# Six buffers for gathered expert rows in place of eight, and query weights in the memory of the other two

## The chip, the cores and the metric

The kernel runs on one core of one Trainium2 chip. The metric is the device time of one execution in microseconds. A NeuronCore has a matrix engine (TensorE, PE in the profile), a vector engine (VectorE, DVE), a scalar engine (ScalarE, ACT), GpSimd (POOL) and SyncE (SP). The last two issue most of this kernel's transfers; all transfers of the core run on the same 16 DMA engines. On-chip memory has 128 partitions.

## What is computed

One block with convolution, windowed attention and a retrieval of experts ("peer"), followed by two further blocks with attention and feed-forward parts, all on 256 tokens of width 1024 in float32. The part that the change touches is the expert retrieval:

```python
q = (h @ w_pq).reshape(B, S, PEER_HEADS, 2, PEER_DHALF)      # 8 heads, 2 x 128
sc = jnp.einsum("bshcd,hcnd->bshcn", q, sub_keys)            # 128 keys per half
s_top, i_top = lax.top_k(sc, 16)
# all 16 x 16 sums of the two halves, of which the best 16 name 16 experts
a = gelu(jnp.einsum("ced,cd->ce", u_emb[idx], hx))           # one dot per expert
out = jnp.einsum("ce,ced->cd", g * a, v_emb[idx])            # weighted sum of rows
```

Each token picks 8 x 16 = 128 experts out of 16384. For each it needs a row of `u_emb` and a row of `v_emb`, 1024 floats each, which lie side by side in one array `uv`.

## The kernel before

**Rows of experts.** Tokens lie on the partitions, in two tiles of 128. For each tile and each of its 128 expert slots, POOL issues one indirect DMA (line 751) that brings 128 rows of 2048 floats (1 MB) into one of `NROWS = 8` buffers of `gath`, a view of the memory `pool` from offset 0. These are 256 gathers, numbered n in the code, here called rows. DVE forms the dot of the first half with the token's normed activations (line 2242). ACT handles two rows at a time: gelu (L1660), product with the gate (L1664), a diagonal matrix from each coefficient (L1670). PE multiplies the diagonal with the second half of the row and sums in PSUM (L1221). When PE is through with row n, `row_spent` rises, and POOL may issue gather n + 8 (`wait_spent(gp, n - NROWS)`).

**What stands between the rows.** Each group of 16 rows belongs to one head of one tile. While they are worked, DVE selects the experts of the head two groups later, in nine steps. ACT computes the exponentials of the gates once per group, which needs another table than gelu. PE projects queries and scores of heads 2 to 7 at fixed rows, written in `QUERY_SLOTS`: projections at rows 0, 8, 19, 30, 42 and 54, scores at 2, 14, 25, 36, 48 and 60. Heads 0 and 1 are done ahead of the stage. In the second tile PE also runs three token projections of the next block (`TOKEN_SLOTS`, rows 159, 183 and 207 in all) on the first tile's result.

**Weights.** SP streams all weights as chunks of up to 2 MB, in the order of `CHUNKS`, into a ring of three slots (line 698). Chunk n is loaded when chunk n - 3 has had its last use. The query weights are four chunks `pq` 0 to 3, two heads each. `pq` 2 is outside the ring: it is loaded early into four places that are free at that time. In the ring the order around the stage is convout 0 and 1, wout 0 and 1, pq 0, pq 1, pq 3, va, cqkv 0, cqkv 1, qa. `LAST_USE` names the fill after which each slot may be reused: for pq 0 the query of head 1, tile 1; for pq 1 the query of head 3 (row 8); for pq 3 that of head 7 (row 54).

**The start of the stage.** The experts of the first head come in two halves of eight. POOL waits for the first eight (`first_ranks`) ahead of gather 0. Buffers 0 to 3 lie below the copies of the output projection's weights in `pool` (`f_hi`, from offset 8432 on), buffers 4 to 7 over them. So POOL waits for the last output fill (`wout`, 1, 1) ahead of gather `ROWS_BELOW_WEIGHTS = 4`. The convolution's outputs `y_hi` and `y_lo` use `pool` from 0 to 4336 and are last read by the fill (`convout`, 1, 1).

Of the kernel before, what the change touches and what calls it, by code (L numbers as in the profile page):

```python
# [25 lines left out]
D = 1024  # L26
KD = D // P
# [15 lines left out]
LARGE = 3.0e38  # L43
TABLE_SCALE = 8.0
UNITS = NT * PH
NROWS = 8
NDIAG = 4
SELECT_STEPS = 9
SELECT_AT = (0, 2, 3, 5, 7, 8, 10, 12, 13)
# [27 lines left out]


EARLY_QUERY = 2


def chunk_list():
    out = [(("glu", i), 4096) for i in range(4)] + [(("q1", i), 4096) for i in range(2)] + [(("kv1", 0), 2048)]
    out += [(("gate", i), 4096) for i in range(4)]
    out += [(("attno", i), 4096) for i in range(2)] + [(("convout", i), 4096) for i in range(2)]
    out += [(("wout", i), 4096) for i in range(2)]
    out += [(("pq", i), 4096) for i in range(4) if i != EARLY_QUERY]
    out += [(("va", 0), 4096), (("cqkv", 0), 4096), (("cqkv", 1), 4096), (("qa", 0), 4096), (("ka", 0), 4096),
            (("kpe_uq", 0), 3328), (("uq_ukv", 0), 3584), (("evout", 0), 4096), (("evout", 1), 4096)]
    for layer in range(2):  # L90
        if layer:
            out += [(("uz", 0), 4096), (("vz", 0), 4096), (("qd", 0), 4096), (("kd", 0), 4096), (("vd", 0), 4096),
                    (("ws", 0), 1024), (("odout", 0), 4096), (("odout", 1), 4096)]
        out += [(("gu%d" % layer, i), 4096) for i in range(KF // 2)]
        out += [(("down%d" % layer, i), min(4, KF - 4 * i) * D) for i in range(-(-KF // 4))]
    return out
# [67 lines left out]
               30: ("pq", 5), 36: ("sc", 5), 42: ("pq", 6), 48: ("sc", 6), 54: ("pq", 7), 60: ("sc", 7)}  # L164
QUERY_LAG = 4
QUERY_COPY_AFTER = {n + (QUERY_LAG if n else 0): fill for n, fill in QUERY_SLOTS.items()}
ROWS_BELOW_WEIGHTS = 4
SELECT_FIRST_AT = (7, 8, 9, 10, 11, 12, 13, 14, 15)
TOKEN_CHUNKS = (("va", 0), ("cqkv", 0), ("cqkv", 1))
NORM_SLOT = 15  # L170
# [47 lines left out]
FILL_NO = {name: n for n, name in enumerate(FILLS)}  # L218
# [102 lines left out]
        self.scale, self.table, self.sinks, self.column = scale, table, sinks, column  # L321


def build(nc, stream, early_query, consts, t5const, params, rows, keys_in, late_rows, x_in, positions, t5_in, rpb_in, uv, out):
    with ExitStack() as ctx:
        def sb(name, shape, dt=F32):
            return ctx.enter_context(nc.sbuf_tensor(name, shape, dt))
# [1 line left out]
        def sem(name):  # L329
            return ctx.enter_context(nc.semaphore(name))  # L330
# [12 lines left out]
        pool = sb("pool", [P, 16384])  # L343
# [99 lines left out]

        qpT = view(att, 5120, 2, 2, S)
        keys = tab[:, :, :].rearrange("p h j -> p (h j)")[:, 0:2048].rearrange("p (m n) -> p m n", n=NKEYS)
        gath = view(pool, 0, NROWS, 2 * D)
        scores = view(att, 0, NT, 2 * PH * NKEYS)
        cand = att[:, 4096:4096 + TOPK * TOPK]
        first_cand = att[:, 1024:1024 + TOPK * TOPK]
# [38 lines left out]
        bank_filled = sem("bank_filled")  # L488
# [18 lines left out]
        row_landed = sem("row_landed")  # L507
        keys_landed = sem("keys_landed")
        early_query_landed = sem("early_query_landed")
        pos_landed = sem("pos_landed")  # L510
        t5_landed = sem("t5_landed")
        rpb_landed = sem("rpb_landed")
# [171 lines left out]
        @block.sync  # L684
        def _(sp):
            for t in range(NT):
                sp.dma_start(x[:, t, :], x_in[P * t:P * t + P, :]).then_inc(x_landed[t], 16)
            sp.dma_start(cst[:, :], consts).then_inc(const_landed, 16)
            sp.dma_start(par[:, :], params).then_inc(param_landed, 16)
            for n, (name, width) in enumerate(CHUNKS):  # L690
                if n >= NSLOT:
                    before = CHUNKS[n - NSLOT][0]
                    if before in LAST_PART:
                        wait_part_used(sp, *LAST_PART[before])
                    else:
                        sp.wait_ge(bank_filled, FILL_NO[last_use(before)] + 1)
                src = stream[CHUNK_AT[n]:CHUNK_AT[n + 1]].rearrange("(p w) -> p w", p=P)
                sp.dma_start(ring[:, n % NSLOT, 0:width], src).then_inc(chunk_landed[n % NSLOT], 16)
                if name == ("wout", 0):
                    sp.wait_ge(bank_filled, FILL_NO["attno", 1, 1] + 1)  # L700
                    sp.wait_ge(t5_stored, 16)
                    sp.wait_ge(rpb_stored, 16)
                    for c, piece in enumerate(query_pieces):
                        sp.dma_start(piece, early_query[:, 1024 * c:1024 * c + 1024].rearrange("p (k n) -> p k n", k=2)
                                     ).then_inc(early_query_landed, 16)
            for t in range(NT):
                sp.wait_ge(out_ready, t + 1)
                sp.dma_start(out[P * t:P * t + P, :], xn[:, t, :]).then_inc(out_stored, 16)
            sp.wait_ge(out_stored, 16 * NT)
# [69 lines left out]
        def _(pe):  # L779
# [404 lines left out]
            def query(kind, head):  # L1184
                dst = begin((kind, head))
                if kind == "pq":
                    if head // 2 == EARLY_QUERY:
                        pe.wait_ge(early_query_landed, 16 * len(query_pieces))
                        w = [query_pieces[k // 2][:, k % 2, :] for k in range(KD)]
                    else:  # L1190
                        chunk = wait_chunk(pe, ("pq", head // 2))[:, 0:4096].rearrange("p (k n) -> p k n", k=KD)
                        w = [chunk[:, k, :] for k in range(KD)]
# [51 lines left out]
            w = wait_chunk(pe, ("kpe_uq", 0))  # L1244
# [1261 lines left out]
```

## Time and profile before

| | us |
|---|---|
| three runs, median | 1607.2 |
| lowest, highest | 1601.48, 1609.42 |
| the profiled execution | 1604.03 |
| its span in the trace | 1602.1 |
| PE, DVE, ACT, POOL busy in the span | 1447.7, 1017.3, 646.3, 312.3 |
| moved by DMA | 428.59 MB, 268 GB/s on average |

The page lists busy time by engine, then the span in 40 slices of 40 us, each digit being tenths of a slice, then the chain of work that ended last and the costliest groups. Here the longest items of the chain are the landings of gathers (`pool<-uv,experts`, 19% of the span) and the three kinds of split matmuls (L933 to L935, 12% each). Idle time of an engine that is not the bound costs nothing; what matters of each stage is the wait that ends last in it.

### The profile page before, as it was taken

Reading aid. Unit: us, or ns where it says so; the run is one execution under the profiler, and the core shown is the slowest. Engines: PE = TensorE matmul, PEld = TensorE weight load, DVE = VectorE, ACT = ScalarE, POOL = GpSimd, SP = SyncE. Lnnn points to the kernel's source line nnn. Section 1 sums busy time; section 2 is a strip of 40 time slices with the busy share of each in tenths; the row PEclk is TensorE's granted clock in tenths of the full one; section 3 lists DMA queues with packets and bytes.
Section 4 is the critical chain, followed back from the end, with each engine's and each line's share of the span. In section 5 each row is a group of like instructions: output and inputs, shape, how many; then the busy total and the mean of one; then the engine's idle time right before and its main releaser. Section 6 shows DMA issues by size and latency. Waiting matters only on the chain.

```text
span 1602.1 us, 16913 instructions
## 1 busy us (share of the span) xinstructions
PE 1447.7 (90%) x6102; PEld 1002.6 (63%) x6102; DVE 1017.3 (63%) x1989; ACT 646.3 (40%) x1313; POOL 312.3 (19%) x298
## 2 busy tenths in 40 slices
PE   8998898989977777797987779989999999999998
PEld 6987897745533332333333237767888889878886
DVE  6999976767667777777665543346555455565553
ACT  4423662333333334433333224454444345544442
POOL 2000001144444444434434410400000000000000
PEclk9999999999999999999999999999999999999999
DMA  7546455999999999999999955413454444145451
GB/s 296 205 164 137 121 216 217 395 398 418 412 421 421 419 420 420 420 397 421 411 410 417 421 223 191 148 73 130 185 206 162 182 166 164 73 190 203 165 201 62
DMA packets 52212, 428.59 MB, mean 268 GB/s; under 512 B 6696, under 2 KB 6840, under 8 KB 10144
## 3 DMA queue, kind: packets, MB, share of 16 engines
q0 software_dynamic: 40464, 279.18, 43.7%
q1 hardware_dynamic: 11664, 148.33, 24.4%
q8 instruction: 49, 0.80, 0.2%
q14 instruction: 35, 0.29, 0.0%
HBM read 422.49 MB, written 4.98 MB: 267 GB/s over the span
## 4 chain that ended last, share of the span: by engine, by line
PE 62%; DMA 20%; DVE 10%; ACT 5%; issue 2%; POOL 0%; SPq 0%; DVEq 0%; ACTq 0%; POOLq 0%
DMA pool<-uv,experts 19%; PE psum L933 12%; PE psum L935 12%; PE psum L934 12%; PE psum L800 11%; PE psum L1221 10%; DVE pool L2242 3%; PE psum L834 2%; DVE pool L2010 2%; PE psum L880 1%; DVE ring_lo L1834 1%; ACT diag L1670 1%; ACT xn L1316 1%; DVE att L1811 1%; ACT coef L1664 1%
## 5 line engine op out<-in xcount | busy, mean ns | idle before, releaser
L1221 PE MATMUL psum<-pool,diag 128*128 128x512 f32 x1024 | 482.5, 621 | 109.9 <-ACT diag L1670 109.6
L1221 PEld LDWEIGHTS psum<-pool,diag 128*128 128x128 f32 x1024 | 194.7, 197 | 388.6 <-issue 213.0
L2242 DVE CUSTOM_DVE_ANT_0 pool<-pool,xn 128x1024 f32<-128x1024 f32 x256 | 313.4, 1226 | 195.8 <-DMA pool<-uv,experts 193.8
L751 POOL DMA_INDIRECT pool<-uv,experts x256 | 281.4, 1099 | 514.4 <-PE psum L1221 366.4
L1834 DVE TENSOR_TENSOR ring_lo<-ring,w_hi 128x2048 fp32r<-128x2048 f32 x76 | 174.0, 2292 | 114.0 <-ACT w_hi L1412 113.9
L1660 ACT ACTIVATE acts<-dots 128x2 f32<-128x2 f32 x128 | 26.0, 203 | 366.6 <-DVE dots L2242 366.4
L1412 ACT ACTIVATE w_hi<-ring 128x2048 fp32r<-128x2048 f32 x76 | 144.4, 1908 | 65.1 <-PE psum L935 36.0
L933 PE MATMUL psum<-w_hi,h_hi 128*128 128x512 f32 x400 | 161.2, 403 | 2.5 <-DVE ring_lo L1834 0.9
L934 PE MATMUL psum<-ring_lo,h_hi 128*128 128x512 f32 x400 | 157.2, 393 | 0.0
L935 PE MATMUL psum<-w_hi,h_lo 128*128 128x512 f32 x400 | 156.1, 390 | 0.0
L800 PE MATMUL psum<-hT,ring 128*128 128x256 f32 (+1 forms) x544 | 116.8, 376 | 0.8 <-issue 0.8
L800 PEld LDWEIGHTS psum<-hT,ring 128*128 128x128 f32 x544 | 100.2, 201 | 16.5 <-issue 3.1
L2010 DVE SCALAR_TENSOR_TENSOR pool<-pool,par 128x256 f32<-128x256 f32 x240 | 98.3, 486 | 0.2
L1670 ACT ACTIVATE diag<-cst,coef 128x128 f32<-128x128 f32 x256 | 89.6, 394 | 9.3 <-PE psum L1221 5.0
L933 PEld LDWEIGHTS psum<-w_hi,h_hi 128*128 128x128 f32 x400 | 75.2, 188 | 21.5 <-issue 3.1
L935 PEld LDWEIGHTS psum<-w_hi,h_lo 128*128 128x128 f32 x400 | 75.2, 188 | 18.6
L934 PEld LDWEIGHTS psum<-ring_lo,h_hi 128*128 128x128 f32 x400 | 74.9, 187 | 15.3
L933 PE MATMUL psum<-w_hi,gu_hi 128*128 128x512 f32 x176 | 70.1, 398 | 0.0
L934 PE MATMUL psum<-ring_lo,gu_hi 128*128 128x512 f32 x176 | 69.0, 392 | 0.0
L935 PE MATMUL psum<-w_hi,gu_lo 128*128 128x512 f32 x176 | 68.7, 390 | 0.0
L1664 ACT ACTIVATE coef<-acts,gates 128x1 f32<-128x1 f32 x256 | 61.4, 287 | 4.2
L1312 ACT ACTIVATE pool<-psum 128x512 f32<-128x512 f32 (+1 forms) x47 | 23.1, 505 | 88.7 <-PE psum L800 62.1
(327 smaller groups left out, 2156.1 us busy)
## 6 DMA issues: line engine op xcount, KB each, us to landing
ring<-stream SPq DMA_DIRECT2D x65, 2048.0 KB, 7.7
pool<-uv,experts POOLq DMA_INDIRECT x256, 12.5
ring<-stream SPq DMA_DIRECT2D x3, 1024.0 KB, 4.8
t_scratch<-tab POOLq DMA_DIRECT2D x1, 2048.0 KB, 56.3
rpb_scratch<-tab POOLq DMA_DIRECT2D x1, 1792.0 KB, 23.1
ring<-stream SPq DMA_DIRECT2D x1, 1792.0 KB, 8.1
row<-rows POOLq DMA_DIRECT2D x1, 1672.0 KB, 11.3
ring<-stream SPq DMA_DIRECT2D x1, 1664.0 KB, 6.6
```

The costliest lines, as they stand in the source:

```text
L751: gp.indirect_dma_start(out=gath[:, n % NROWS, :], out_offset=None, in_=uv, in_offset=bass.IndirectOffsetOnAxis(ap=experts[:, n:n + 1], ax ...
L800: last = nc.tensor.matmul(dst, lhsT, rhs, start=(i == 0), stop=(i == len(pairs) - 1))
L933: nc.tensor.matmul(dst, lhsT[0], rhs[0], start=start, stop=False)
L934: nc.tensor.matmul(dst, lhsT[0], rhs[1], start=False, stop=False)
L935: return nc.tensor.matmul(dst, lhsT[1], rhs[0], start=False, stop=stop)
L1221: last = nc.tensor.matmul(psum[:, RB + half, :], diag[:, n % NDIAG, :], gath[:, n % NROWS, D + 512 * half:D + 512 * half + 512], start=k = ...
L1412: nc.scalar.activation(part_high(layer, q), part_raw(layer, q), ACT.Copy).then_inc(hi_split, 1)
L1664: ins = nc.scalar.activation(coef[:, b, j:j + 1], acts[:, b, j:j + 1], ACT.Copy, scale=gates[:, n:n + 1])
L1670: nc.scalar.activation(diag[:, n % NDIAG, :], ident, ACT.Copy, scale=coef[:, b, j:j + 1]).then_inc(diag_ready, 1)
L1834: V.tensor_tensor(part_low(layer, q), part_raw(layer, q), part_high(layer, q).bitcast(F32), ALU.subtract).then_inc(lo_split, 1)
L2010: ins = V.scalar_tensor_tensor(y[:, m, :], src, tap, y[:, m, :], ALU.mult, ALU.add)
L2242: ins = V.tensor_tensor_reduce(out=row_u, in0=row_u, in1=xn[:, n // SLOTS, :], scale=1.0, scalar=0.0, op0=ALU.mult, op1=ALU.add, accum_out ...
```

## The change

`NROWS` becomes 6: `gath` starts at offset 4096 of `pool`, and the first 4096 columns of it, the place of two buffers, hold the query weights `pq` 3 of heads 6 and 7. These leave the ring. They come as an input of their own and are loaded by SP right behind chunk pq 0, after a wait for (`convout`, 1, 1). PE takes them from there for heads 6 and 7 and waits for their own semaphore. `ROWS_BELOW_WEIGHTS` becomes 2, since only two buffers now lie below the copies of the weights. The number of DMAs and of computing instructions is the same. One SP wait is added; one ring position fewer is used, which shifts all later chunks by one slot.

```diff
-NROWS = 8
+NROWS = 6
...
+ROW_QUERY = 3
...
-    out += [(("pq", i), 4096) for i in range(4) if i != EARLY_QUERY]
+    out += [(("pq", i), 4096) for i in range(4) if i not in (EARLY_QUERY, ROW_QUERY)]
...
-ROWS_BELOW_WEIGHTS = 4
+ROWS_BELOW_WEIGHTS = 2
...
-        gath = view(pool, 0, NROWS, 2 * D)
+        gath = view(pool, 2 * 2 * D, NROWS, 2 * D)
+        row_weights = pool[:, 0:2 * 2 * D]
...
                 sp.dma_start(ring[:, n % NSLOT, 0:width], src).then_inc(chunk_landed[n % NSLOT], 16)
+                if name == ("pq", 0):
+                    sp.wait_ge(bank_filled, FILL_NO["convout", 1, 1] + 1)
+                    sp.dma_start(row_weights, row_query).then_inc(row_query_landed, 16)
                 if name == ("wout", 0):
...
                     if head // 2 == EARLY_QUERY:
                         pe.wait_ge(early_query_landed, 16 * len(query_pieces))
                         w = [query_pieces[k // 2][:, k % 2, :] for k in range(KD)]
+                    elif head // 2 == ROW_QUERY:
+                        pe.wait_ge(row_query_landed, 16)
+                        w = [row_weights[:, 512 * k:512 * k + 512] for k in range(KD)]
```

## Rows read from the trace of the kernel before

**Rows 1.** The page, DMA share and rate in 40 slices of 40 us.
```profile
DMA  7546455999999999999999955413454444145451
GB/s 296 205 164 137 121 216 217 395 398 418 412 421 421 419 420 420 420 397 421 411 410 417 421 223 191 148 73 130 185 206 162 182 166 164 73 190 203 165 201 62
```

**Rows 2.** Windows: length, busy PE, PEld, DVE, ACT, POOL, then PEclk, DMA, GB/s.
```profile
247.00:262.00 15.00, 14.23 (x82) 11.63 (x82) 6.41 (x24) 3.75 (x11) 0.00 (x0) 1.00 0.00 1
...
505.30:512.00 6.70, 5.74 (x7) 2.52 (x8) 4.93 (x17) 2.54 (x9) 1.35 (x1) 0.50 1.01 421
...
450.00:940.00 490.00, 388.45 (x828) 156.89 (x828) 335.28 (x811) 174.21 (x532) 207.23 (x190) 0.96 1.01 416
```

**Rows 3.** Line 751, the gathers issued from 880 to 926 us.
```profile
L751 POOL DMA_INDIRECT pool<-uv,experts x19: 943/943/1802, 881.1 to 926.0; - x19
...
DMA to landing us min/median/max: 12.2/12.7/13.5
```

**Rows 4.** Timeline of DVE, start and us; the dots of rows 249 and 253.
```profile
926.24 1.23 DVE L2242 CUSTOM_DVE_ANT_0 pool<-pool,xn 128x1024 f32<-128x1024 f32 x1 [1.15 <-DMA pool<-uv,experts]
...
936.22 1.23 DVE L2242 CUSTOM_DVE_ANT_0 pool<-pool,xn 128x1024 f32<-128x1024 f32 x1 [1.14 <-DMA pool<-uv,experts]
```

**Rows 5.** Timeline of PE, one pair of rows in an undisturbed stretch.
```profile
923.73 3.70 PE L1221 MATMUL psum<-pool,diag 128*128 128x512 f32 x8 [1.29 <-ACT diag L1670]
```

**Rows 6.** Timeline of POOL, the eighth and the ninth gather.
```profile
275.69 1.14 POOL L751 DMA_INDIRECT pool<-uv,experts  x1 [0.30 <-issue]
298.76 0.94 POOL L751 DMA_INDIRECT pool<-uv,experts  x1 [21.94 <-PE psum L1221]
```

**Rows 7.** Line 751, the two gathers issued at 298.8 and 300.0 us.
```profile
L751 POOL DMA_INDIRECT pool<-uv,experts x2: 941/942/942, 298.8 to 300.0; - x2
...
DMA to landing us min/median/max: 5.5/6.7/7.8
```

**Rows 8.** SP's queue: first start, us to the last; then one issue by line.
```profile
227.76 11.71 SPq L698 DMA_DIRECT2D ring<-stream  x2
262.41 26.12 SPq L698 DMA_DIRECT2D ring<-stream  x3
317.83 0.33 SPq L698 DMA_DIRECT2D ring<-stream  x1
438.86 0.33 SPq L698 DMA_DIRECT2D ring<-stream  x1
...
L698 SPq DMA_DIRECT2D ring<-stream x1: 328/328/328, 268.0 to 268.0; - x1
```

**Rows 9.** Timeline of DVE, the dots of rows 59 and 60.
```profile
442.35 1.22 DVE L2242 CUSTOM_DVE_ANT_0 pool<-pool,xn 128x1024 f32<-128x1024 f32 x1 [0.92 <-DMA pool<-uv,experts]
...
449.12 1.23 DVE L2242 CUSTOM_DVE_ANT_0 pool<-pool,xn 128x1024 f32<-128x1024 f32 x1 [5.54 <-DMA pool<-uv,experts]
```

**Rows 10.** The chain of work: start, us; query projections (first, last), first token projection.
```profile
310.90 6.91 PE psum L800 x32
...
431.92 6.91 PE psum L800 x32
...
702.48 6.87 PE psum L800 x16
```

**Rows 11.** Line 751, the gather issued at 711.3 us.
```profile
L751 POOL DMA_INDIRECT pool<-uv,experts x1: 1351/1351/1351, 711.3 to 711.3; - x1
...
DMA to landing us min/median/max: 7.6/7.6/7.6
```

**Rows 12.** Start of the group at row 80: ACT, PE, and that gather's landing.
```profile
503.76 1.28 ACT L1660 ACT_TABLE_LOAD   x1 [2.52 <-DVE dots L2242]
...
506.26 9.14 PE L1221 MATMUL psum<-pool,diag 128*128 128x512 f32 x14 [3.09 <-ACT diag L1670]
...
L751 POOL DMA_INDIRECT pool<-uv,experts x1: 1346/1346/1346, 510.3 to 510.3; - x1
...
DMA to landing us min/median/max: 9.1/9.1/9.1
```

More of the change, by code:

```diff
@@ L321, in __init__, with build @@
         self.scale, self.table, self.sinks, self.column = scale, table, sinks, column
-def build(nc, stream, early_query, consts, t5const, params, rows, keys_in, late_rows, x_in, positions, t5_in, rpb_in, uv, out):
+def build(nc, stream, early_query, row_query, consts, t5const, params, rows, keys_in, late_rows, x_in, positions, t5_in, rpb_in, uv, out):
     with ExitStack() as ctx:
@@ L509, in build @@
         early_query_landed = sem("early_query_landed")
+        row_query_landed = sem("row_query_landed")
         pos_landed = sem("pos_landed")
@@ L2494 @@
     arrays = {
-        "stream": stream, "early_query": parts["pq", EARLY_QUERY], "consts": consts, "t5const": t5, "params": params, "rows": rows, "late_rows": late,
+        "stream": stream, "early_query": parts["pq", EARLY_QUERY], "row_query": parts["pq", ROW_QUERY],
+        "consts": consts, "t5const": t5, "params": params, "rows": rows, "late_rows": late,
         "x_in": a["x"].reshape(S, D), "positions": a["positions"].reshape(NT, P).T, "t5_in": a["t5_bias_2"],
```

## Prediction

> **What bounds the kernel now.** First the page's slices: between about 270 us and 940 us the sixteen DMA engines are at nine tenths or more and move 395 to 425 GB/s, before and after that they are half idle [rows 1]. The windows say the same more sharply: from 450 to 940 us the DMA share is 1.01 while PE is busy for 388 of 490 us, DVE for 335 and ACT for 174; in the 15 us from 247 to 262, just ahead of the stage, DMA moves nothing [rows 2]. So the expert stage is bound by transfers. 256 gathers of 1 MB go one after another, and one row of experts becomes usable every 2.5 us: DVE's dots, each waiting for a landing, start at 926.24 and 936.22, four rows apart, 9.98/4 = 2.495 us [rows 4]. PE needs 3.70 us for two rows and then stands 1.29 us waiting for ACT [rows 5].
>
> The reader should see next that the DMA engines never run dry because gathers are issued long before they are needed. With eight buffers a gather takes 12.7 us (median; 12.2 to 13.5) from issue to landing late in the stage [rows 3]; it stands behind others. Gather n waits until row n-8 has been through PE. So 8 x 2.495 = 19.96 us is one row's time in a buffer: 12.7 to 13.5 us from issue to landing, and the other 7.2 to 6.4 us from landing to the next issue (dot, gelu, diagonal, PE). The even row of a pair waits for its odd partner, so it is held 7.2 us and its successor lands after 12.7; the odd one is held 6.4 and its successor lands after 13.5. How short can issue to landing be? Two gathers went into an empty queue at 298.8 and 300.0: 5.5 and 7.8 us [rows 7]. I call 5.5 us the floor: below it the engines stand still.
>
> **The change part by part.**
>
> *Six buffers.* The cycle falls to 6 x 2.495 = 14.97 us. The hold stays, so issue to landing falls by 4.99 us, to 7.7 (even) and 8.5 us (odd). That is above the floor by 2.2 and 3.0 us. With nothing disturbing the stage six would be enough. But whatever holds PE up by more than that now idles the DMA engines, and since they are the bound this is never won back. Under eight the margin was 7.2 to 8.0 us, more than any single disturbance.
>
> *The disturbances, first kind.* Eight times PE does something else between two rows: five query projections of 32 matmuls (6.91 us each, ahead of rows 8, 19, 30, 42 and 54) and three token projections of 16 (6.87 us, ahead of rows 159, 183, 207) [rows 10]. Ahead of an even row 1.3 us of it fall into PE's usual wait, so buffers come free 5.6 us late; ahead of an odd row 6.9 us. The trace has the effect already, harmless there: the gather behind the first token projection lands after 7.6 us instead of 13.5 [rows 11]. Cost now: even (8, 30, 42, 54) 5.6 - 2.2 = 3.4 us each, 13.6; odd (19, 159, 183, 207) 6.9 - 3.0 = 3.9 each, 15.6. Sum **+29.2 us**. The single score fills (1.1 us) stay inside the margin.
>
> *Second kind.* At the start of each group of 16 rows ACT loads a table for the exponential and one back for gelu, 1.28 us each. PE then stands 3.09 us, and 14 matmuls take 9.14 us where 8 otherwise take 3.70 [rows 5, 12]: the granted clock is 0.50 just there, the lower of its two levels, 1.2 GHz [rows 2]. The gather issued then lands after 9.1 us instead of 12.7 [rows 12]: 3.6 us late, 1.4 above the margin. The mean clock of 0.96 over 490 us makes 39 us at the lower level, about eight such places at 5 us. Bounds: 0 (the clock falls elsewhere, or the queue was just filled up) and 14 groups x 1.4 = 20 us. I take five places, nearest to the row: **+7 us**.
>
> *Filling the queue again.* The gather of 300.0 landed 3.5 us after the one of 298.8, not 2.5 [rows 7]. If every stall costs this further 1.0 us, nine make 9; if small transfers that now delay rows run in the pauses instead, it is 0 or slightly below. I take **+3 us**.
>
> *The start.* Eight gathers go out from 266.8 to 275.7; the ninth waits 21.94 us for row 0 to be through PE [rows 6] and lands at 298.8 + 5.5 = 304.3. With six, the gather that waits there is that of row 6, issued and landing at the same moment; the stream after it is two rows behind: **+5.0 us**. Two rows below the weights' copies instead of four costs nothing: gather 2 goes out at about 269.4, and what it now waits for (the last output fill) had released SP's issue at 268.0, inside the SP row of three issues from 262.41 [rows 8]. Were this fill later, gathers 2 and 3 would wait, with 20 us in hand before row 0 is used.
>
> *The moved weights.* Their 2 MB go out behind the issue at about 239.1 (the second of the SP row of 227.76), whose own condition is the wait that is added, so nothing queues behind it: SP's next issue is at 262.41 [rows 8]. They land in the empty stretch [rows 2], 150 us before head 6 is projected. Cost 0; without that idle stretch it would be 5 us of transfer. POOL and the other queues are not passed. PE reads them from another address in the same matmuls: 0. What is saved is found by counting ring loads in the stage. Before: SP issues at 268.0 (third query part), 288.2 (va), 317.8 and 438.9 (cqkv). The ring now carries va at 268.0, cqkv at 288.2 and 317.8, and nothing at 438.9. That last one cost: the dot that waited for its row began 6.77 us after the one before [rows 9], 4.3 more than usual, and 2.1 MB at 418 GB/s are 5.0. **-5.0 us**. The stage's exit is as before; the next ring load waits for va's last use, past the experts.
>
> *Sum.* 29.2 + 7 + 3 + 5.0 - 5.0 = **+39 us**. The profiled execution took 1604.0 us around its span of 1602.1, so its sum is 1643. The median of the three runs is 1607.2, 3.2 above it; against that I forecast **1646 us**.
>
> *A rule that gives another size.* The Trainium skill, page "DMA: Bandwidth & Descriptors", section on the anatomy of one DMA, puts one DMA at 2.0 us fixed plus bytes over 436 GB/s, an estimate of 4.4 us for 1 MB. The row shows 5.5 [rows 7], so the trace does not agree, though one pair of gathers is thin. By that page's figure the floor would be 1.1 us lower and the first kind would cost 20.4 in place of 29.2.
>
> **The rivals.**
>
> *A. A lower floor.* What matters is not how soon a lone gather lands but whether the next has data ready as the last ends. If that needs a lead of only 4.4 us, the margins are 3.3 and 4.1: 4 x 2.3 + 4 x 2.8 = 20.4, groups and refill 2, start and weights cancel: +22, **1629 us**. For it: 7.6 us was still far from any gap [rows 11]. Against: the only landings with no queue took 5.5.
>
> *B. The clock joins in.* A stalled DMA leaves PE idle some 3 us a few rows later; such an idle was followed by the lower clock, and rows then held buffers 3.6 us longer [rows 12]. If most stalls bring this on, each of nine adds 1.4 to 3.6 us; at 1.6, with the full 9 us of refill, 39 + 6 + 9 x 1.6 = +59, **1667 us**. For: same mechanism already at the groups. Against: PE's backlog after a projection covers part of the gap.
>
> *C. Not slower.* The last two buffers were never wanted: POOL and the queue take up a delay of 7 us because landings bunch and PE catches up at 1.85 us a row against 2.5. Price 0 for the disturbances; start and moved weights cancel: **1607**, or 1602 if the two missing rows at the start are also made good. It decides if a gather issued 7 us late still lands in line, that is if the lead may fall to about 1.6 us. Nothing in the trace lands within that.
>
> *D. The weights do not leave the stage* (a transfer of the same size slips in at 438.9): +5 on the forecast, 1651. The order of the ring speaks against it.
>
> **How the numbers follow.** Forecast 0.63, A 0.14, B 0.13, C 0.06, D 0.04. The forecast's own range takes both unknown terms to their ends, +29 (both 0) to +58 (20 and 9). To hold eight in ten the range must take in A and most of B: **1622 to 1666**. Half a per cent (8 us) is about what a measurement tells from no change here. Faster by more needs C with a further gain of 3 us: 0.02. Within it: C and the lowest of A, 0.06. Slower: 0.92.
>
> **What the profile after would show.** Gathers in quiet stretches landing 7.7 to 8.5 us after issue; eight idle stretches of DMA of 3 to 4 us, each six rows after a projection; GB/s of the stage's slices falling from 418 to about 395; the stage some 39 us longer and everything after it equal; three ring loads in place of four between 266 and 940 us; row 6 landing at about 304. If quiet gathers are at the floor, the hold has grown. If the eight places show no gap, A or C is right; if PE's clock is low far more often than at eight places, B. The forecast is wrong at its root if gathers of an undisturbed stretch come slower than 2.5 us with six in flight.

## The result and the profile after

| | before | after |
|---|---|---|
| median, us | 1606.45 (4 runs) | 1672.84 (4 runs) |
| lowest, highest | 1601.48, 1609.42 | 1668.08, 1676.06 |
| the profiled execution | 1604.03 | 1671.83 |
| its span | 1602.1 | 1670.0 |
| last row's dot starts | 941.43 | 1010.68 |

The ratio is 1.0418, with a 95% interval of 1.0397 to 1.0439: 67 us slower, where +39 was forecast, and above the range of 1622 to 1666. The stage's end moved by 69.3 us and the span by 67.9, so all of it lies in the stage. (In after the gather is line 757, the dot L2251, the rows' matmuls L1230, the gates' products L1673, the diagonals L1679.)

The page's slices of the whole span answer to [rows 1]. From the ninth to the 24th, all inside the stage, the rate is 353 to 403 GB/s, and 328 in one, in place of 395 to 425.

```profile
DMA  7446477899999999999899995440445444254541
GB/s 302 185 166 134 120 279 277 319 374 364 362 359 376 375 383 382 367 395 364 328 391 353 397 403 190 157 158 36 187 182 201 164 164 165 101 194 159 202 176 76
```

Windows of after (columns as in [rows 2]): the late stage, and a quiet stretch near its end.

```profile
450.00:1010.00 560.00, 428.20 (x897) 176.83 (x896) 345.90 (x831) 178.72 (x548) 220.84 (x199) 0.93 0.95 376
...
938.00:960.00 22.00, 16.56 (x37) 6.32 (x35) 10.81 (x17) 5.51 (x20) 8.49 (x9) 1.00 1.01 414
```

Against [rows 2] the DMA share is 0.95 in place of 1.01 and PE's granted clock 0.93 in place of 0.96. Even per busy engine less is moved: 376/0.95 is 396 GB/s, where 416/1.01 is 412. So engines are idle, and when busy they are a little slower. The quiet stretch has neither fault: 414 GB/s. The forecast had expected about 395 GB/s for the stage.

The gathers of that stretch (POOL's timeline, with the wait ahead of each; then the line's group, from issue to landing) answer to [rows 3]; PE's pairs there to [rows 5].

```profile
953.80 0.94 POOL L757 DMA_INDIRECT pool<-uv,experts  x1 [2.32 <-PE psum L1230]
955.52 0.94 POOL L757 DMA_INDIRECT pool<-uv,experts  x1 [0.77 <-PE psum L1230]
```

```profile
L757 POOL DMA_INDIRECT pool<-uv,experts x8: 943/943/944, 943.8 to 960.5; - x8
...
DMA to landing us min/median/max: 7.7/8.1/8.5
```

```profile
951.54 3.70 PE L1230 MATMUL psum<-pool,diag 128*128 128x512 f32 x8 [1.28 <-ACT diag L1679]
```

7.7 and 8.5 us, as forecast, and no row is late. The disturbed places are the matter. Behind the first token projection, PE, then POOL, then DVE's dots:

```profile
746.82 7.03 PE L806 MATMUL psum<-ring,hT 128*128 128x512 f32 x16
```

```profile
755.84 1.26 POOL L757 DMA_INDIRECT pool<-uv,experts  x1 [7.64 <-PE psum L1230]
```

```profile
755.06 1.23 DVE L2251 CUSTOM_DVE_ANT_0 pool<-pool,xn 128x1024 f32<-128x1024 f32 x1 [0.69 <-DMA pool<-uv,experts]
...
761.75 1.22 DVE L2251 CUSTOM_DVE_ANT_0 pool<-pool,xn 128x1024 f32<-128x1024 f32 x1 [5.45 <-DMA pool<-uv,experts]
```

PE projects for 7.03 us, the buffer for row 165 comes free only at 755.8, and its dot starts 6.69 us after that of row 164, 4.2 more than the usual 2.49. In between the DMA engines stand still (a window of one us each; DMA share and rate are the last two columns):

```profile
755.00:756.00 1.00, 1.00 (x4) 0.52 (x3) 0.94 (x1) 0.53 (x2) 0.16 (x1) 1.00 0.02 8
756.00:757.00 1.00, 1.00 (x3) 0.41 (x3) 0.29 (x2) 0.01 (x1) 1.00 (x1) 1.00 0.03 8
```

### The profile page after: what moved, and what is told of

Read it like the earlier page. It is cut to its first block, busy times and chain, and to the rows that moved or that the text cites. A ratio compares the mean times of both kernels' runs of the same rounds, so it can differ in the third digit from the quotient of the medians.

```text
span 1670.0 us, 16913 instructions
## 1 busy us (share of the span) xinstructions
PE 1470.9 (88%) x6102; PEld 1012.4 (61%) x6102; DVE 1016.9 (61%) x1989; ACT 646.0 (39%) x1313; POOL 314.0 (19%) x298
## 4 chain that ended last, share of the span: by engine, by line
PE 62%; DMA 19%; DVE 11%; ACT 5%; issue 3%; POOL 0%; SPq 0%; DVEq 0%; ACTq 0%; POOLq 0%
DMA pool<-uv,experts 18%; PE psum L1230 13%; PE psum L939 12%; PE psum L940 11%; PE psum L941 11%; PE psum L806 11%; DVE pool L2251 3%; DVE pool L2019 2%; PE psum L840 2%; DMA ring<-stream 1%; PE psum L886 1%; DVE ring_lo L1843 1%; ACT diag L1679 1%; ACT L1669 1%; ACT coef L1673 1%
## 5 line engine op out<-in xcount | busy, mean ns | idle before, releaser
L1230 PE MATMUL psum<-pool,diag 128*128 128x512 f32 x1024 | 507.5, 649 | 153.0 <-ACT diag L1679 153.0
L2251 DVE CUSTOM_DVE_ANT_0 pool<-pool,xn 128x1024 f32<-128x1024 f32 x256 | 313.5, 1226 | 267.6 <-DMA pool<-uv,experts 266.1
L1230 PEld LDWEIGHTS psum<-pool,diag 128*128 128x128 f32 x1024 | 203.7, 206 | 447.0 <-issue 225.0
L806 PE MATMUL psum<-hT,ring 128*128 128x256 f32 (+1 forms) x480 | 103.1, 376 | 2.3 <-DMA ring<-stream 1.5
L806 PEld LDWEIGHTS psum<-hT,ring 128*128 128x128 f32 x480 | 88.4, 204 | 14.7 <-issue 2.9
L1679 ACT ACTIVATE diag<-cst,coef 128x128 f32<-128x128 f32 x256 | 89.1, 394 | 6.7 <-PE psum L1230 2.5
L1673 ACT ACTIVATE coef<-acts,gates 128x1 f32<-128x1 f32 x256 | 61.4, 287 | 4.2
L1321 ACT ACTIVATE pool<-psum 128x512 f32<-128x512 f32 (+1 forms) x47 | 23.1, 505 | 86.4 <-PE psum L806 59.7
## 6 DMA issues: line engine op xcount, KB each, us to landing
row<-rows POOLq DMA_DIRECT2D x1, 1672.0 KB, 11.1
```

The lines of the kernel that those rows point to most:

```text
L806: last = nc.tensor.matmul(dst, lhsT, rhs, start=(i == 0), stop=(i == len(pairs) - 1))
L1230: last = nc.tensor.matmul(psum[:, RB + half, :], diag[:, n % NDIAG, :], gath[:, n % NROWS, D + 512 * half:D + 512 * half + 512], start=k = ...
L1673: ins = nc.scalar.activation(coef[:, b, j:j + 1], acts[:, b, j:j + 1], ACT.Copy, scale=gates[:, n:n + 1])
L1679: nc.scalar.activation(diag[:, n % NDIAG, :], ident, ACT.Copy, scale=coef[:, b, j:j + 1]).then_inc(diag_ready, 1)
L2251: ins = V.tensor_tensor_reduce(out=row_u, in0=row_u, in1=xn[:, n // SLOTS, :], scale=1.0, scalar=0.0, op0=ALU.mult, op1=ALU.add, accum_out ...
```

## Where the 67 us lie

I call **lead** the time from a gather's issue to the landing of the row before it: how long ahead of its turn a gather is asked for. A landing normally follows the one before by 2.49 us; what is over that is the row's **loss**. Over rows 1 to 255 the losses sum to 28.4 us before and 96.8 after, 68.4 apart. By place:

| rows | before | after |
|---|---|---|
| 1 to 7, the start | 6.3 | 12.9 |
| 8 to 63, five query projections | 16.5 | 27.1 |
| 64 to 159, one projection at the very end (159) | 1.6 | 27.7 |
| 160 to 223, the effect of three token projections | 3.1 | 25.7 |
| 224 to 255 | 1.0 | 3.4 |

By lead, rows 8 to 255 of after (count, mean loss, sum), and the mean loss of the same class with five buffers (experiment below):

| lead, us | rows | mean loss | sum | five buffers |
|---|---|---|---|---|
| under 1 | 5 | 4.0 | 20.2 | 3.5 |
| 1 to 3 | 10 | 1.7 | 16.6 | 1.2 |
| 3 to 4 | 17 | 1.0 | 17.7 | 1.0 |
| 4 to 5 | 31 | 0.7 | 22.7 | 0.7 |
| 5 to 5.5 | 23 | 0.16 | 3.6 | 0.15 |
| 5.5 and over | 162 | 0.02 | 3.2 | 0.08 |

A floor of 5.5 us from issue to landing means a row is late only if the lead is under 5.5 - 2.5 = 3.0 us. Those 15 rows lost 36.8 us, where the forecast had 39.2 for all its holes. The 71 rows with a lead of 3 to 5.5 us lost another **44.0 us**, and the forecast had nothing for them. The quiet rows of after have a lead of 5.2 and 6.1: already at the edge.

The same classes for the kernel before: two rows under 3 us lose 1.5, eleven from 3 to 5.5 us lose 6.5, and the other 235 lose 14.3, of which 6.6 stand at rows 15, 60 and 61, where a ring load of 2 MB shares the engines. So the 68.4 us between the two traces are 6.6 at the start, 35.3 at leads under 3, 37.5 at 3 to 5.5, and 11.1 less at the longer leads.

## Experiments

All ratios below are to the kernel before on the same chip. Losses by place are those of the one execution that was traced; where it lies over 5 us from the median of its kernel, this is said. Executions of one six-buffer kernel lie 4 to 20 us apart, and the next run, which differs little from after, loses 23.1 us at rows 64 to 159 where after loses 27.7: a difference of 5 us in that figure says little. The first runs ask what part of the change costs.

**Six buffers alone, seven alone.**

```diff
-NROWS = 8
+NROWS = 6
```

> One part of the change alone: the kernel before with six buffers; the weights of heads 6 and 7 stay in the ring. Two theories of the missing 29 us. Feed: a gather must be issued about 5.5 us ahead of the landing before it to leave no hole, not 3 us, so the margin under six buffers is almost nothing; all of the loss is that of the buffers. Then this kernel loses what the whole change lost plus the transfer at 438.9 us: 66 + 5, about +71 us on before (67 to 77), with the same holes at the group starts. Rival (the moved weights or the new ring order cost something themselves): it is nearer to before than the change, +66 or less.

Measured 1671.07 us, ratio 1.0435 [1.0388, 1.0482]: as after, whose interval overlaps. That is +62 to +77 us, which does not tell the two expectations apart. Rows 54 to 63, where this kernel still loads 2 MB into the ring, lose 7.4 us in place of after's 4.8. The moved weights give a few us at most; within the interval the two buffers are the whole change.

> The kernel before with seven buffers, weights in the ring. A gather then has 2.5 us more lead than with six: quiet gathers land 10.2 and 11.0 us after issue. Floor of 5.5 us, as the prediction had it: the eight projections cost 1 us each, the group starts nothing, the start 2.5: +6 to +11 us. Feed: 7.5 us is what a gather needs behind others, the margin is 2.7 to 3.5 instead of 4.7 to 5.5, projections cost about 2.5 each and the low-clock group starts 1: +18 to +28 us.

Measured (`NROWS = 7`) 1618.95 us, ratio 1.0086 [1.0069, 1.0103], about 14 us. That lies between the two readings (+6 to +11 and +18 to +28): the floor charges too little, and the second reading, a need of 7.5 us from issue to landing, too much. Losses stand behind the projections (rows 166, 167: 2.9; 190, 191: 3.1), and rows 64 to 159 lose 2.6 only. The step from eight to seven costs 14 us and the next one 52: the cost rises steeply once quiet rows stand at the edge.

**No table loads.** After, with ACT's second table left out.

```diff
-                nc.scalar.activation(g, g, ACT.Exp).then_inc(best_exp_ready, 1)
+                nc.scalar.activation(g, g, ACT.Exp if unit < 2 else ACT.Copy).then_inc(best_exp_ready, 1)
```

> The changed kernel, with the exponential of the gates left out from the third group on (a copy takes its place, so the gates are no softmax any more and the result is another one). ACT then loads no tables in the stage, and PE is not kept waiting at the group starts. The holes of rows 64 to 158, where no projection runs, sum to 28 us in the changed kernel. Both theories: what starts them is the pair of table loads; they fall below 6 us and the stage is 25 to 40 us shorter than the change's. Rival (six in flight are too few even undisturbed): the holes stay above 15 us.

Measured 1662.33 us (1653.23 to 1673.5), ratio 1.0333 [1.0294, 1.0371], 10 us of median better than after, where both theories had 25 to 40. The traced execution was the slowest of the four, and rows 64 to 159 lose 22.9 us in it, as in the run with six buffers alone. So the table loads account for some 10 us of the 67 and not for most of the holes; how many of the holes are gone in the quicker executions is not known. The same edit with eight buffers:

> The kernel before with the gates' exponential replaced by a copy from the third head on, so that ACT loads no second table in the stage (left out: the exponential of most gates, so the output differs). The same edit took 10 us off the six-buffer kernel. Lead: with eight buffers the leads are 8 to 11 us, a table load of 1.3 us takes none below 5.5: no change, 1602 to 1606. Rival, the tables cost the same with eight: 1594 to 1599.

Measured 1604.33 us, ratio 0.9995 [0.9982, 1.0008]. What costs some 10 us with six buffers costs nothing with eight.

**Warm PE at the groups' starts.** Ten matmuls on zero weights ahead of each group's first row.

```diff
+                    if k and k % TOPK == 0:
+                        for _ in range(FILLERS):
+                            nc.tensor.matmul(psum[:, RB, 0:S], zeros[:, :], cst[:, 0:S], start=False, stop=False)
                     pe.wait_ge(diag_ready, n + 1)
```

> The changed kernel; at each group start but the first of a tile PE runs ten matmuls of 128x256 with zero weights into the open sum, 2.2 us, inside the 3.1 us in which it waits for ACT. The table loads stay, only PE is not idle. Clock theory: the lower clock after that idle is what makes the hold long; without it the holes of rows 64 to 158 fall from 28 to under 8 us and the kernel gains 25 us or more. Feed: the wait for ACT itself (1.8 us more than usual) already exceeds the margin, the clock adds the rest; the holes fall to 12 to 20 us and the kernel gains 8 to 20 us.

Measured 1694.51 us, ratio 1.056 [1.0536, 1.0585], 22 us worse than after, which neither expectation had. (The traced execution is the quickest of the four.) The timeline of PE behind the first token projection says why:

```profile
745.95 7.03 PE L809 MATMUL psum<-ring,hT 128*128 128x512 f32 x16
752.82 1.88 PE L1237 MATMUL psum<-pool,diag 128*128 128x512 f32 x4
754.53 4.48 PE L1234 MATMUL psum<-cst,zeros 128*128 128x256 f32 x20
758.85 9.61 PE L1237 MATMUL psum<-pool,diag 128*128 128x512 f32 x22
```

The ten cost 4.5 us, and ahead of row 160 PE has no idle time: they stand right behind the pause that makes the hole. The losses behind the projections grew from 30 to 47 us. Meanwhile the clock did rise, and the losses of rows 64 to 159 fell only from 27.7 to 20.7 us. Windows of this kernel, then of after:

```profile
450.00:600.00 150.00, 125.78 (x324) 60.32 (x324) 98.93 (x247) 47.08 (x148) 66.18 (x56) 0.98 0.97 386
600.00:720.00 120.00, 92.41 (x224) 41.55 (x224) 82.60 (x208) 46.44 (x129) 48.78 (x45) 0.97 0.97 384
```

```profile
450.00:600.00 150.00, 112.54 (x252) 49.20 (x250) 94.79 (x235) 46.21 (x146) 64.35 (x54) 0.93 0.94 372
600.00:720.00 120.00, 91.61 (x182) 37.71 (x183) 81.02 (x206) 45.34 (x125) 48.85 (x44) 0.89 0.98 377
```

**The lead as theory.** It came out of the runs above, so it had to forecast others. Five buffers set the two readings furthest apart:

```diff
-NROWS = 8
+NROWS = 5
```

> The kernel before with five row buffers and nothing else changed. Two readings of the six-buffer runs. Lone-gather floor (the step of the prediction): a gather needs 5.5 us, so in a quiet stretch (rows 230 to 239) a buffer's round is 6.7 us of hold, 0.3 of issue and 5.5 of transfer, 12.5 us for five rows or 2.50 us a row, and the whole is about 125 us slower than before, near 1731. Lead: with the previous landing less than about 5.5 us after the issue, some of the DMA engines run short, as the six-buffer runs show (0.2 us lost a row at a lead of 5, 0.85 at 4 to 4.5, 1.4 at 3). A round of five rows leaves a lead of 4c - 7.0 us at c us a row, which closes at c of 2.85 to 2.95: a quiet stretch at that rate, and the whole about 190 us slower, near 1797.

Measured 1791.88 us (1784.04 to 1799.74), ratio 1.1151 [1.1094, 1.1208]: 1797 was the lead's figure, 1731 the floor's. In the window from 1030 to 1110, which has no projection, 26 dots start, one per 3.1 us. That is worse than the 2.85 to 2.95 expected of a quiet stretch; nothing is quiet there, so the total came out closer than its parts. The table above shows the loss at a given lead to be nearly the same with five buffers as with six from 3 us up, and somewhat smaller below (1.2 against 1.7 at 1 to 3 us).

```profile
1030.00:1110.00 80.00, 54.41 (x102) 21.63 (x101) 31.62 (x55) 20.67 (x68) 27.65 (x25) 0.88 0.87 326
```

**More lead with the same six buffers.** PE multiplies half the columns, so rows come free sooner.

```diff
+                    cols = 512 if k in (0, SLOTS - 1) else 256
                     for half in range(2):
-                        last = nc.tensor.matmul(psum[:, RB + half, :], diag[:, n % NDIAG, :],
-                                                gath[:, n % NROWS, D + 512 * half:D + 512 * half + 512],
+                        last = nc.tensor.matmul(psum[:, RB + half, 0:cols], diag[:, n % NDIAG, :],
+                                                gath[:, n % NROWS, D + 512 * half:D + 512 * half + cols],
```

> The kernel after, but PE multiplies only the first 256 of each 512 columns of a row, save the first and the last row of a tile (left out: half of each weighted row sum, so the output differs). A row is then released 0.9 us sooner if it is the first of its pair and 1.8 us sooner if the second, with the same six buffers, the same transfers and the same projections. Lead: quiet rows get a lead of 6.1 and 7.9 us in place of 5.2 and 6.1, beyond the 5.5 from which nothing is lost, so the holes of rows 64 to 159 fall from 27.8 us to under 12, and the whole from 1673 to about 1641. Lone-gather floor: about half of that, 15 us off, 1658. Rival, six in flight are too few whatever the lead: no gain, 1665 to 1675.

Measured 1644.65 us, ratio 1.0236 [1.0203, 1.0269]: the lead's figure (1641), not the floor's (1658). Rows 64 to 159 lose 13.1 us, a little over the 12 expected. The window and one pair of rows show a thing that I had not foreseen:

```profile
450.00:720.00 270.00, 154.67 (x449) 107.94 (x448) 188.18 (x467) 95.67 (x285) 117.45 (x101) 0.76 0.99 399
```

```profile
938.88 3.78 PE L1231 MATMUL psum<-pool,diag 128*128 128x256 f32 x8 [1.21 <-ACT diag L1680]
```

PE has less to do and its granted clock falls to 0.76; at the lower level a pair of half rows takes 3.78 us, as a whole one does at full clock. So much of the stage had no more lead than after. But a low clock could no longer hold a row longer than usual, and in a backlog PE caught up faster. The gain is that of both.

**Split projections.** Each of the eight projections in two halves, two rows apart.

```diff
                     if n in QUERY_SLOTS:
-                        query(*QUERY_SLOTS[n])
+                        parted = n and QUERY_SLOTS[n][0] == "pq"
+                        query(*QUERY_SLOTS[n], halves=(0,) if parted else (0, 1))
+                    if n - 2 in QUERY_SLOTS and n > 2 and QUERY_SLOTS[n - 2][0] == "pq":
+                        query(*QUERY_SLOTS[n - 2], halves=(1,))
```

> The kernel after with each of the eight projections that stand between rows split into two halves, the second half two rows later, so that PE's pause is twice 3.5 us with two rows between in place of 6.9 at once. Lead: the row behind a whole projection has a lead of 0 to -1 us and costs 4 to 4.5; behind a half it has 2 to 3 and costs 1.4 to 1.8, twice; sum about 1.5 us less at each of eight places and fewer low-clock stretches: 12 to 18 us faster than after, 1655 to 1661. Rival, the loss goes by the work that PE does between the rows and not by the pause: as after, 1668 to 1676.

Measured with six 1661.72 us, ratio 1.0361 [1.0318, 1.0403], 11 us better than after, just past the weak end of what the lead theory expected (1655 to 1661) and clear of the rival's 1668 to 1676.

> The kernel before with seven row buffers and the eight projections split in halves two rows apart. With seven whole, 1619 was measured, 13 to 15 us over before, of which some 16 us of holes stand six to eight rows behind the projections. Lead: quiet rows have a lead of 7.7 to 8.6 us here; a pause of 6.9 us leaves 2 and costs 1.8 and 1.3, a pause of 3.5 leaves about 5 and costs 0.2, so of the 16 us about 6 to 8 go: 1611 to 1614. Rival, the loss goes by the sum of PE's work between rows: no change, 1617 to 1620.

Measured with seven 1611.45 us, ratio 1.005 [1.0033, 1.0067]. The two intervals for seven, whole and split, do not overlap: 7.5 us of 14 are won back by shorter pauses, and one buffer (1 MB) costs 0.5%.

> The kernel before, eight buffers, with the same split of the eight projections. Rows 166, 191 and 214 and rows 15, 16, 27, 28 and 39 lose some 9 us together in the trace of before. Lead: at most 4 us of that goes, 1602 to 1605. Rival, these losses are not the projections' (instruction fetches or the ring's loads): no change, 1604 to 1608. A loss of a few us would say that the second switch of the weights and the later scores cost more than the shorter pause gives.

Measured with eight 1603.25 us, ratio 0.999 [0.9975, 1.0005]. No difference can be told. No version here beats the kernel before.

**Is the low clock a cause?** Of the losses of after, 30.0 us stand at the two rows that take the buffers freed right behind a projection, and 44.8 us at 40 rows which wait for a row that ran at the lower clock. PE's timeline shows the sequence at the group of row 80: an idle PE, then 24 matmuls in 12.26 us, where three quick pairs would take 11.1.

```profile
522.34 3.70 PE L1230 MATMUL psum<-pool,diag 128*128 128x512 f32 x8 [1.17 <-ACT diag L1679]
529.14 12.26 PE L1230 MATMUL psum<-pool,diag 128*128 128x512 f32 x24 [3.10 <-ACT diag L1679]
```

PE idles over 2.5 us ahead of rows 64, 70, 76; 80, 86, 92; 96, 102, 108; 112, 118, 124; 128, 134: six rows apart, the number of buffers. From the landing of row 6 to the stage's end the clock of after is low 28 times, 95 us in all; before, 10 times and 44 us. A loop suggests itself: a hole idles PE, the clock falls, the rows come free late, the next hole comes six rows on. First trial, two zero matmuls behind each pair (`if k % 2:` behind `row_spent`):

> The kernel after with two matmuls on zero weights (128x256, 0.43 us each at full clock) behind each pair of rows, where PE waits 1.3 us anyway; the rows are released ahead of them. In the trace of after 30.0 us of the holes stand right behind the eight projections, as the prediction had it, and 44.8 us, at 40 rows, stand six or seven rows behind a row whose four matmuls took over 2.4 us, that is at the lower clock. Clock theory (the loop: a hole idles PE, the clock falls, the rows are released late, the next hole comes six rows on): the granted clock of the stage rises from 0.93 to 0.98 or more, the 44.8 us fall below 15, and the whole to 1635 to 1650; the sum over the projections stays or grows by a few us, since PE catches up more slowly. Rival (the low clock is only company of the holes, which come from too short a lead): the clock rises and the time stays at 1668 to 1680. A third case: PE still idles in the holes and the clock falls all the same, then nothing is told apart.

Measured 1673.37 us, ratio 1.0408 [1.037, 1.0447]. The losses behind low-clock rows fell from 44.8 to 22.2 us, and others rose by more (those behind the projections from 30 to 38; this execution is the slowest of the four). PE had 0.9 us less per pair to catch up with, which I take for the reason.

> The same matmuls on zero weights and also the eight projections split in halves two rows apart. Split alone took 11 us off (1661.7). Clock theory: both add up, since shorter pauses make shorter holes and a warm PE releases the rows on time: 1622 to 1638. Rival: near 1662.

Measured 1664.62 us, ratio 1.0381 [1.0348, 1.0415], as the split alone. Second trial, zero matmuls only where PE had stood idle in the trace of after:

```diff
+FILLERS = {n: 5 for n in (64, 80, 96, 112, 144, 176, 192, 224, 240, 14, 36, 48, 60, 166, 190, 214)}
+FILLERS.update({n: 3 for n in (70, 86, 102, 118, 134, 150, 182, 198, 230, 246)})
...
+                    for _ in range(FILLERS.get(n, 0)):
+                        nc.tensor.matmul(psum[:, RB, 0:S], zeros[:, :], cst[:, 0:S], start=False, stop=False)
                     pe.wait_ge(diag_ready, n + 1)
```

> The kernel after with matmuls on zero weights (128x256, 0.45 us each) only at 26 rows ahead of which PE stood idle for 2 to 4 us in the trace of after: five ahead of each of 16 rows (2.2 us), three ahead of each of 10 (1.3 us). Clock theory: the low stretches of the stage (28, 95 us) fall to under 12, the holes behind low-clock rows from 44.8 to under 20 us, nothing is given back in backlogs, and the whole is 1645 to 1658. Rival, the short lead makes the same holes from any small delay: the clock rises and the whole stays at 1666 to 1678.

Measured 1666.19 us (1658.92 to 1671.71), ratio 1.0372 [1.033, 1.0413]. The clock was low for 41 us instead of 95, the losses behind such rows fell to 18.6 us, but the whole by 7 us of median only, with intervals that overlap. My clock theory (1645 to 1658) fell; the rival's figure (1666 to 1678) holds. It does not isolate the price of the low clock: the zero matmuls take PE's time too, and the losses behind the projections grew from 30 to 34 us. Window of this kernel, then of the next:

```profile
450.00:1000.00 550.00, 446.58 (x1078) 202.55 (x1076) 342.53 (x827) 176.99 (x543) 224.71 (x198) 0.97 0.96 378
```

```profile
450.00:1000.00 550.00, 452.73 (x1109) 204.84 (x1108) 351.30 (x847) 153.88 (x539) 220.65 (x201) 0.98 0.96 388
```

> The same, and the gates' exponential replaced by a copy from the third head on, so that ACT loads no second table (left out: the exponential of most gates, so the output differs). The table loads alone were worth 10 us of median with six buffers and nothing with eight. Clock theory: with both gone rows 64 to 159, where no projection stands, lose under 8 us in place of 27.7, and the whole is 1630 to 1648. Rival, six in flight are too few even for undisturbed rows: over 18 us there, 1655 to 1670.

Measured 1662.0 us (1654.84 to 1667.15), ratio 1.0368 [1.0342, 1.0394]. Rows 64 to 159 lose 11.0 us in the profiled execution, between the two expectations; the total is the rival's. That execution (span 1653.0) was the quickest of the four, so its 11.0 flatters.

> The same again with the eight projections split in halves two rows apart; the last of the three disturbances halved (left out: the exponential of most gates). Split alone took 11 us off. Clock theory: 1620 to 1638, the rest of the distance to before being the start (7 us) and the halves. Rival: 1645 or more.

Measured 1652.18 us, ratio 1.0286 [1.0253, 1.0319]: with the clock low for 44 us as before, the tables gone and each pause halved, 46 us of 67 remain. Rows 64 to 159 lose 22.1 us in the traced execution, the slowest of the four, so this overstates. Of these, 15.6 are lost at rows that wait neither for a projection nor for a row at the lower clock, most of them with a lead of 4.6 to 5.3 us. At such a lead small delays suffice; which delays these were was not traced.

**What a short lead does in the engines.** This is counted from the packet records of the traces (8 KB each, 128 to a gather), from the landing of row 6 to that of row 255. "Idle" is the length less all packets' time over 16 engines; "slow" are a gather's packets of over 0.33 us, where one normally takes 0.309 to 0.313; their excess is what they take over 0.309. (The idle time of before comes out below nothing since the records of packets overlap a little.)

```
                      length   idle   slow packets   their excess / 16
before (8)             644.7   -2.6            314                 6.3
seven                  658.4    8.2            666                11.5
after (6)              704.7   37.9           2336                40.0
after, short rows      683.3   27.5           1676                26.5
five                   823.7  108.1           4270                84.3
```

Between before and after lie 60 us. Idle engines make 40.5 of them and slow packets 34; from this go 7 since an ordinary packet takes 0.309 us in place of 0.313, and 7 for other transfers no longer made there. Slow packets begin at the same lead as the losses: in after, with a lead under 5 about 20 to 30 of the 128, most of them of 0.35 to 1.0 us, at 7 or more about three. Two durations bound why 3.0 us of lead are too few. A gather's first packet starts 1.6 us after its issue (at 298.8 in the trace of before, at 298.2 and 359.2 in that of after). And in undisturbed stretches the 16 engines finish one gather at different times, the first a median 2.4 us ahead of the landing in before and 1.7 in after. So, as an estimate, the first engine runs dry at a lead below 3.3 to 4.0 us. By the Trainium skill, page "DMA: Bandwidth & Descriptors", section on why a DMA increments its semaphore by 16, only the full count of all engines says that a transfer has landed; the trace agrees, with 16 updates of the semaphore to a gather, spread over those 1.7 to 2.4 us. Why packets are slow already between 4 and 5.5 us of lead was not settled.

## Why the prediction was wrong, step by step

- **What bounds the kernel**: right. The stage is bound by transfers, and all 67 us arose in it.
- **Six buffers, quiet rows**: right, 7.7 and 8.5 us.
- **The floor of 5.5 us and the margins of 2.2 and 3.0**: the step that failed. 5.5 us is about the time of one gather when the engines have run dry (5.6 to 5.8 us at the issues of 359.2, 391.5, 825.3 and 894.1 in after), and I took it for the time that a gather in a stream needs. A stream is kept at 2.49 us a row only with a lead of 5.5 us, that is 8 us from issue to landing. Quiet rows had -0.3 and +0.6 us of margin. 44.0 us are lost at leads of 3 to 5.5 us, where the forecast had none (before: 6.5).
- **The evidence stood in the rows quoted.** Contrary to what I wrote, the queue of [rows 7] was not empty: the gather of row 7, issued at 275.7, landed at 301.0, that is 2.2 us after row 8 was issued, and row 8 landed 3.3 us after it, 0.8 late.

```profile
L751 POOL DMA_INDIRECT pool<-uv,experts x1: 1135/1135/1135, 275.7 to 275.7; - x1
...
DMA to landing us min/median/max: 25.3/25.3/25.3
```

The second gather had a lead of 4.3 us and landed 1.0 us late. I booked that as "refill", +3 us in all. Behind the second query projection of before it is there again. Of two gathers issued at 353.2 and 355.0 the first took 5.8 us and landed at 359.0, the second 7.7 and landed at 362.7: a lead of 4.0, 1.2 us late.

```profile
L751 POOL DMA_INDIRECT pool<-uv,experts x2: 946/982/1018, 353.2 to 355.0; - x2
...
DMA to landing us min/median/max: 5.8/6.7/7.7
```

- **Eight projections, +29.2**: the two rows behind each lose 30.0 us in after, single places 2.2 to 5.5. But before already lost 6.8 there, which I had not subtracted: +23. That 30.0 lies so near 29.2 is partly luck.
- **Group starts, +7, and refill, +3**: about 26 us more in rows 64 to 159 alone. Most of what was mis-sized is here, since small delays are what a margin of nothing turns into holes. The upper bound of 20 us was itself taken from the wrong margin.
- **The start, +5.0**: 6.6. Row 6 was issued at 298.2 as expected, but took 7.8 us into an empty queue, not 5.5 (gather 6 and 7 of after):

```profile
L757 POOL DMA_INDIRECT pool<-uv,experts x2: 939/940/940, 298.2 to 299.9; - x2
...
DMA to landing us min/median/max: 7.8/8.2/8.6
```

In the other six-buffer runs that first landing took 5.5 to 8.1 us. One row was thin for a floor.
- **The moved weights, -5.0**: the ring's loads are as counted, none between 323.6 and the stage's end. The saving at row 60 is there (before loses 4.9 at rows 60 and 61), but with six buffers about half of it is left (7.4 against 4.8 us at rows 54 to 63), and six buffers alone, without it, are no slower than after beyond the noise.

```profile
227.68 11.71 SPq L701 DMA_DIRECT2D ring<-stream  x2
239.43 0.43 SPq L704 DMA_DIRECT2D pool<-row_query  x1
262.34 61.24 SPq L701 DMA_DIRECT2D ring<-stream  x4
```

- **The rivals.** A's question was the right one (must the next have data ready as the last ends?), but its answer, 4.4 us from issue to landing, was on the wrong side of 5.5: some 8 are needed. B's price (1667) was closest, and its sign, a clock that is low far more often, was seen. But bringing the low clock back to what it was before gave back about 7 of 67 us: B was nearly right on the sum, but by these runs most of the loss has another reason; the clock's own share was not isolated. C is refuted: the gather issued late at 755.8 did not land in line. So is D, since no ring load is issued between 323.6 us and the stage's end. The estimate of 4.4 us for one transfer by the Trainium skill, page "DMA: Bandwidth & Descriptors", section on the anatomy of one DMA, does not agree with the traces, where no gather landed in under 5.3 us.

## What to carry to other kernels

A ring of buffers is long enough when, in the quiet stretches, each transfer is issued early enough to cost nothing *and* the longest delay still fits above that; the first has to be read from transfers in a stream by their lead, not from one issued when the engines have run dry. Plot the delay of each landing against its lead in the trace at hand before buffers are taken away: the few rows with a short lead are the only ones that tell. Near that edge the cost is not that of the large pauses alone; every small one starts to count, and edits that cost nothing with buffers to spare (a table load, a whole pause of 7 us in place of two halves) cost some 10 us each with six.

## What the runs showed of the hardware that I had not expected

- 1 MB gathers (128 rows of 8 KB) need to be issued about 5.5 us before the previous one lands to follow at 2.49 us. At a lead of 4 to 5 us each loses 0.7 us and at 3 to 4 us 1.0, with five and six buffers alike; at 1 to 3 us it is 1.2 with five and 1.7 with six. (With seven buffers only 27 rows have a lead under 5.5 us: 0.6 at 4 to 5 us, 1.5 at 1 to 3.)
- In such rows of after 20 to 30 of the 128 packets take mostly 0.35 to 1.0 us instead of 0.31.
- A PE with half the work in the rows ran at a granted clock of 0.76 in place of 0.91 (450 to 720 us), and the kernel was 28 us faster: a granted clock is not a measure of the time. The PE of that run was busy for 155 of the 270 us, that of after for 204.
